# One core, three transformer layers in split float32: other order of the work in the seams, in the gated recurrence and at the start

## Chip, core and metric

The kernel runs on one core of one Trainium2 chip. The metric is the device time of one execution in microseconds (us); the figure for a kernel is the median of its runs.

## What is computed

256 tokens of width 1024 (x) go through three blocks. Block one: a gated linear recurrence (HGRN2) and a squared-ReLU MLP. Block two: differential attention on shared keys and values, and an MLP. Block three: latent attention beside a short convolution, a gated MLP, and a gated per-layer embedding. All is float32. The core of the reference, cut:

```python
h = x + rms_norm(hgrn2_mixer(rms_norm(x, a_norm_pre), a_w_in, lb, ...), a_norm_post)
h = h + rms_norm(squared_relu_mlp(rms_norm(h, mlp_norm_pre[0]), w_up, w_down), mlp_norm_post[0])
k_sh, v_sh = shared_kv(h, kv_norm, w_kv)
# differential attention + MLP in the same pattern, then the third block in the same pattern

# the recurrence, per head, per chunk of 64 tokens:
b = cumsum(log_f); o_inter = (q * exp(b)) @ state
scores[t, s] = sum_k q[t, k] * exp(b[t, k] - b[s, k]) * k[s, k]   # s <= t
o = o_inter + scores @ v
state = exp(b_last) * state + (k * exp(b_last - b)).T @ v
```

## The kernel before

Every large product is made in three parts. A float32 matrix is split into a high part (rounded by ScalarE, in fp32r) and a low part (what is left, made by VectorE), and TensorE sums high x high, low x high and high x low. A weight matrix comes in units of 256 output columns; each unit is loaded in two halves of 512 rows (a quantum: 128 x 1024 numbers). For each quantum SyncE issues a 512 KB DMA into `w_raw`, ScalarE copies it to `w_hi` (line 1350), VectorE subtracts (`w_lo`, line 1899), TensorE uses it. There are 4 raw and 5 converted slots; `raw_in`, `hi_ready`, `lo_ready` and `w_used` are the counters that pass a slot on. Each engine runs its own list in program order; the lists are written out by hand, and nothing else sets the order.

TensorE's inner loop is `quantum` (line 600). Its form "feat" makes one record of 512 columns (a high weight tile against the high and low parts of x, which lie side by side) and one of 256 columns (low weight tile); the form "one_bank" makes three records of 256 columns. A record in the trace is one MATMUL; a product of plain float32 operands shows as two records.

Three places matter here.

The seams. After each of six row-normalised products (`a_post`, `m0_post`, `b_post`, `m1_post`, `mix_post`, `f_post`) the residual stream `h` is renewed tile by tile (8 tiles of 128 rows): VectorE in `post` (line 2024) weighs, adds and makes the low part of the next product's input (`xs`, line 2035), ScalarE makes the high part (line 1442), and TensorE starts the next product tile by tile for two units at once. Until the first tile is there it runs seven products whose result nobody reads (`keep_streaming`, line 777). For tile 0 the high records (`high_records`) of both units come first and wait for the high part alone; the low ones (`low_records`) follow. From tile 1 on, all records of a tile wait for `xs_ready`, the low part. After the eight tiles TensorE sums the squares for the norm of the old entry in two places (`sums("kv_b")`, `sums("f_pre")`); these squares are folded on VectorE (`fold_squares`, `fold_again`), after it has converted two more weight quanta.

The recurrence. The 64 x 64 decays of a chunk are built over levels of blocks of 1, 2, 4 ... 64 tokens. For four heads at a time (a quad) there are nine steps: two on the undecayed q (even and odd tokens), six on decayed q (`hqd`), one for the pair of chunks. A step is 8 products `hk` x q with 64 columns (the last: 4 with 128), and stands behind one weight quantum: steps 0 to 8 behind quanta 9 to 17, steps 9 to 17 behind quanta 18 to 26 (`step`, line 833; `take_step`, line 2182). VectorE takes a step's scores under a mask into `acc` (lines 2201 and 2208) and decays q; GpSimd decays k and multiplies the forget gates (`fprod`).

The start. x comes in two halves; TensorE turns the first into PSUM, runs three products on a table that comes from memory (`keep_streaming(3, bank=2)`, after a wait for `tab_in`), and then turns the second. The first two units follow, with their parts mixed; then `setup_rest` (line 797) with the sum for the first norm and small products for tables; then quantum 4.

Of the kernel before, what the change touches and what calls it, by code (L numbers as in the profile page):

```python
# [8 lines left out]
F32 = mybir.dt.float32  # L9
F32R = mybir.dt.float32r  # L10
I32 = mybir.dt.int32
U32 = mybir.dt.uint32
# [29 lines left out]
STEPS = 8  # L42
T_FREQ = T_LEVEL + STEPS * CHUNK
# [6 lines left out]
def shape_tables():  # L50
# [8 lines left out]
    for n in range(STEPS):  # L59
        if n < 2:  # L60
            mask = (s // 2 == c) & (s % 2 <= n) if n else s == 2 * c
        else:
            b = 2 ** (n - 1)
            mask = (s // (2 * b) == c // b) & (s % (2 * b) < b)
        t[:, T_LEVEL + n * CHUNK:T_LEVEL + (n + 1) * CHUNK] = mask
# [99 lines left out]
HGRN_QUANTA = 32  # L165
AHEAD_FROM = 9
FIRST_STEP, QUAD_STEPS = 9, 9
# [44 lines left out]
def layered_kernel(nc, a, out):  # L212

    ctx = ExitStack()
    with ctx:
# [57 lines left out]
        hq = over("hq", [P, HEADS, S], F32, 0)  # L273
        hk = over("hk", [P, HEADS, S], F32, K8)
        hqd = over("hqd", [P, HEADS, S], F32, 2 * K8)
# [110 lines left out]
        lvl_scored, lvl_taken = sem("lvl_scored"), sem("lvl_taken")  # L386
        oh_ready, oh_squared, oh_ms, oh_guess = sem("oh_ready"), sem("oh_squared"), sem("oh_ms"), sem("oh_guess")
# [57 lines left out]
        def _(sp):  # L445
# [39 lines left out]
            for n in range(4):  # L485
                for which in range(2):
                    for part in range(2):
                        load("f0", (2, 0), 2 * n + which, part,
                             rows(a["a_w_in"][0], 4 * P * part, 4, D * (1 - which) + 256 * n, 256))
                        if n + which + part == 0:  # L490
                            load_x(1)
# [79 lines left out]
        def _(pe):  # L571
            mm = nc.tensor.matmul

            def high_records(s, x, kind, pset):

                hi, lo = w_hi[:, s, 0:2 * P], w_lo[:, s, 0:2 * P]
                for n in range(2):
                    w = slice(n * P, (n + 1) * P)
                    o_ap = ps[:, 2 * pset + n, 0:S] if kind == "feat" else ps[:, pset, n * S:(n + 1) * S]
                    mm(o_ap, hi[:, w], x[:, 0, 0:S], start=(kind == "feat" or n == 0), stop=False)  # L580
                    mm(o_ap, lo[:, w], x[:, 0, 0:S], start=False, stop=False)

            def low_records(s, x, kind, pset):

                for n in range(2):
                    o_ap = ps[:, 2 * pset + n, S:2 * S] if kind == "feat" else ps[:, pset, n * S:(n + 1) * S]
                    mm(o_ap, w_hi[:, s, n * P:(n + 1) * P], x[:, 0, S:2 * S], start=False, stop=False)

            def tile_zero(name, u, x, kind, psets):

                for b in range(2):
                    pe.wait_ge(lo_ready, 2 * (u + b) + 1)
                    if b == 0:
                        pe.wait_ge(xs_hi, XS0[name] + 1)
                    high_records(slot_of(u + b, 0), x, kind, psets[b])
                pe.wait_ge(xs_ready, XS0[name] + 1)
                for b in range(2):
                    low_records(slot_of(u + b, 0), x, kind, psets[b])
# [64 lines left out]
            def first_two_by_tile(name, xname, x, waits, after, between={}):  # L663
# [3 lines left out]
                tile_zero(xname, u, x, "feat", [(p + b) % 2 for b in range(2)])  # L667
                for k in range(1, KT):
                    for b in range(2):
                        if k == 4:  # L670
                            pe.wait_ge(lo_ready, 2 * (u + b) + k // 4 + 1)
                        if b == 0:
                            waits(k, 1)
# [2197 lines left out]
```

## Time and profile before

| | us |
|---|---|
| median of 3 runs | 1008.73 (1008.53 to 1009.54) |
| the profiled execution's own time | 1008.68 |
| its span (first to last instruction) | 1006.9 |
| TensorE matmul busy | 989.4 (98%) |
| VectorE / ScalarE / GpSimd busy | 742.1 / 554.5 / 74.0 |
| DMA | 166.47 MB, mean 165 GB/s |

Times in the rows below are from the span's start. A matmul's end is modelled, so records overlap: the pace of a row of like records is read from start to start, not from the length of one. The number in brackets behind a row is idle time of its engine before it, and what ended it.

### The profile page before, as it was taken

The page shows a single profiled execution, that of the slowest core. Times are in us where ns is not written, and L with a number is a line of the kernel's source. Part 1 is how long each engine was busy: PE and PEld are TensorE (multiplying, and loading weights), DVE is VectorE, ACT ScalarE, POOL GpSimd, SP SyncE. Part 2 cuts the span into 40 slices and gives each one's busy share as a digit, 9 for nine tenths or more (in the row PEclk, how much of TensorE's full clock was granted, in tenths as well). Part 3 has the DMA queues.
Part 4 walks back from the last instruction along what each step waited for, and adds up shares of the span by engine and source line. Part 5 has one row for each costly group of instructions (what it writes and reads, how often), then busy time and mean ns, then how long its engine had stood idle before and what let it go on. Part 6 is the DMA issues. An engine that isn't in the chain of part 4 may idle for free.

```text
span 1006.9 us, 16557 instructions
## 1 busy us (share of the span) xinstructions
PE 989.4 (98%) x6605; PEld 898.8 (89%) x6605; DVE 742.1 (74%) x1115; ACT 554.5 (55%) x819; POOL 74.0 (7%) x81
## 2 busy tenths in 40 slices
PE   7999999999999999999999999999999999999998
PEld 7999998888888989898888888999998788888897
DVE  5887677977764498766987844479777987776776
ACT  5943256655554475755655544455556665556444
POOL 6323101000201000001000201000001000000000
PEclk9999999999999999999999999999999999999999
DMA  8643435566656836435476565626526467665551
GB/s 262 189 133 114 126 112 161 161 204 182 192 183 187 259 110 197 137 115 154 141 218 186 172 199 184 183 76 177 180 85 187 127 182 202 185 186 181 177 166 42
DMA packets 164716, 166.47 MB, mean 165 GB/s; under 512 B 6784, under 2 KB 162832, under 8 KB 164640
## 3 DMA queue, kind: packets, MB, share of 16 engines
q1 hardware_dynamic: 162752, 163.47, 53.0%
q0 software_dynamic: 1056, 1.16, 0.5%
q8 instruction: 53, 0.87, 0.4%
q10 hardware_dynamic: 832, 0.79, 0.3%
q14 instruction: 23, 0.19, 0.1%
HBM read 163.79 MB, written 1.08 MB: 164 GB/s over the span
## 4 chain that ended last, share of the span: by engine, by line
PE 87%; DVE 7%; issue 2%; ACT 2%; POOL 1%; DMA 1%; ACTq 0%; DVEq 0%; POOLq 0%
PE ps L633 32%; PE ps L632 16%; PE ps L616 4%; PE ps L617 4%; PE ps L618 4%; PE ps L629 3%; PE ps L862 3%; PE ps L612 3%; PE ps L610 3%; PE ps L611 3%; DVE w_lo L1899 2%; PE ps L630 2%; PE ps L623 1%; PE ps L624 1%; PE ps L625 1%
## 5 line engine op out<-in xcount | busy, mean ns | idle before, releaser
L1899 DVE TENSOR_TENSOR w_lo<-w_raw,w_hi 128x1024 fp32r<-128x1024 f32 (+3 forms) x318 | 379.1, 1200 | 138.4 <-ACT w_hi L1350 136.7
L1350 ACT ACTIVATE w_hi<-w_raw 128x1024 fp32r<-128x1024 f32 x302 | 317.6, 1054 | 207.9 <-PE ps L633 94.3
L633 PE MATMUL ps<-xs,w_hi 128*128 128x512 f32 x840 | 296.5, 396 | 0.0
L632 PE MATMUL ps<-xs,w_lo 128*128 128x256 f32 x840 | 235.1, 280 | 2.0 <-DVE xs L2035 1.5
L633 PEld LDWEIGHTS ps<-xs,w_hi 128*128 128x128 f32 x840 | 157.7, 188 | 35.1
L633 PE MATMUL ps<-us,w_hi 128*128 128x512 f32 x498 | 176.3, 397 | 0.0
L632 PEld LDWEIGHTS ps<-xs,w_lo 128*128 128x128 f32 x840 | 158.3, 188 | 4.9 <-DVE xs L2035 2.1
L632 PE MATMUL ps<-us,w_lo 128*128 128x256 f32 x498 | 139.9, 281 | 0.0
L633 PEld LDWEIGHTS ps<-us,w_hi 128*128 128x128 f32 x498 | 93.6, 188 | 22.7
L616 PE MATMUL ps<-xs,w_hi 128*128 128x256 f32 x376 | 108.9, 290 | 1.2 <-DVE xs L2035 1.1
L617 PE MATMUL ps<-xs,w_hi 128*128 128x256 f32 x376 | 106.3, 283 | 0.0
L618 PE MATMUL ps<-xs,w_lo 128*128 128x256 f32 x376 | 106.3, 283 | 0.0
L632 PEld LDWEIGHTS ps<-us,w_lo 128*128 128x128 f32 x498 | 93.5, 188 | 0.3
L1357 ACT ACTIVATE tmp<-ps 128x512 f32<-128x512 f32 x75 | 44.5, 594 | 76.5 <-PE ps L633 76.4
L1927 DVE TENSOR_TENSOR mo<-ps,tmp 128x512 f32<-128x512 f32 x75 | 51.6, 688 | 41.3 <-ACT tmp L1357 41.3
L616 PEld LDWEIGHTS ps<-xs,w_hi 128*128 128x128 f32 x376 | 72.0, 191 | 2.8 <-DVE xs L2035 1.5
L2810 POOL TENSOR_TENSOR sq<-sq 128x512 f32<-128x512 f32 x12 | 20.1, 1672 | 716.6 <-ACT sq L1408 522.7
L617 PEld LDWEIGHTS ps<-xs,w_hi 128*128 128x128 f32 x376 | 72.0, 192 | 0.1
L618 PEld LDWEIGHTS ps<-xs,w_lo 128*128 128x128 f32 x376 | 71.9, 191 | 0.0
L612 PE MATMUL ps<-us,w_lo 128*128 128x256 f32 x172 | 48.3, 281 | 0.0
L610 PE MATMUL ps<-us,w_hi 128*128 128x256 f32 x172 | 48.3, 281 | 0.0
L611 PE MATMUL ps<-us,w_hi 128*128 128x256 f32 x172 | 48.3, 281 | 0.0
(412 smaller groups left out, 1684.2 us busy)
## 6 DMA issues: line engine op xcount, KB each, us to landing
w_raw<-in_mlp_w_up SPq DMA_DIRECT2D x64, 512.0 KB, 4.4
w_raw<-in_mlp_w_down SPq DMA_DIRECT2D x64, 512.0 KB, 3.6
w_raw<-in_a_w_in SPq DMA_DIRECT2D x32, 512.0 KB, 3.8
w_raw<-in_w_gate SPq DMA_DIRECT2D x22, 512.0 KB, 3.8
w_raw<-in_w_up SPq DMA_DIRECT2D x22, 512.0 KB, 4.5
w_raw<-in_w_down SPq DMA_DIRECT2D x20, 512.0 KB, 3.5
w_raw<-in_w_kv SPq DMA_DIRECT2D x16, 512.0 KB, 4.4
w_raw<-in_w_in SPq DMA_DIRECT2D x16, 512.0 KB, 3.9
```

The costliest lines, as they stand in the source:

```text
L610: mm(ps[:, bank, 0:S], hi[:, kk, w], x[:, kt, 0:S], start=first, stop=False)
L611: mm(ps[:, bank, 0:S], hi[:, kk, w], x[:, kt, S:2 * S], start=False, stop=False)
L612: o = mm(ps[:, bank, 0:S], lo[:, kk, w], x[:, kt, 0:S], start=False, stop=last)
L616: mm(ps[:, pset, at], hi[:, kk, w], x[:, kt, 0:S], start=first and n == 0, stop=False)
L617: mm(ps[:, pset, at], hi[:, kk, w], x[:, kt, S:2 * S], start=False, stop=False)
L618: o = mm(ps[:, pset, at], lo[:, kk, w], x[:, kt, 0:S], start=False, stop=last and n == 1)
L632: mm(ps[:, bank, 0:S], lo[:, kk, w], x[:, kt, 0:S], start=False, stop=False)
L633: o = mm(ps[:, bank, :], hi[:, kk, w], x[:, kt, :], start=False, stop=last)
L1350: o = fn(dst, raw, ACT.Copy)
L1357: o = fn(tmp[0:rows_, pset if slot is None else slot, :, :], ps[0:rows_, 2 * pset:2 * pset + 2, S:2 * S], ACT.Copy, scale=scale)
L1899: return v.tensor_tensor(d, x, y, ALU.subtract)
L1927: return v.tensor_tensor(dst, ps[0:rows_, 2 * pset:2 * pset + 2, 0:S], tmp[0:rows_, pset if slot is None else slot, :, :], ALU.add)
```

## The change

1. `two_by_tile` takes the place of `tile_zero` and the loops behind it, in the seams: for every tile, not the first alone, the high records of both units wait for the high part and come first, the low ones wait for the low part. In the form "feat" the record of 512 columns becomes two of 256 for tiles 1 to 7.
2. `keep_streaming` runs six products, not seven, at the six seams.
3. `sums("kv_b")` comes one quantum later and `sums("f_pre")` one quantum later; on VectorE the folds move between the two weight conversions at the seam's end.
4. The recurrence: q and decayed q now lie in one buffer `hq_both`. Ten uses of a PSUM bank in eight steps per quad: two steps hold two uses of 4 products with 128 columns each (even columns from q and odd ones from decayed q; then the odd diagonal from a moved copy of q together with level 2), the others stay as they are. The steps begin behind quantum 10. The first eight units come in the order f0 f1 q0 q1 f2 f3 q2 q3, and ScalarE takes the gates in pairs.
5. The start: three products of 128 columns on the identity that is there already, without the wait for `tab_in`; the first unit goes through all tiles before the second; `setup_rest` comes after quantum 4 and the turning of the first norm's factor after quantum 6. ScalarE and VectorE turn the second half of x before the next weights.

```diff
-                pe.wait_ge(tab_in, 16)
-                keep_streaming(3, bank=2)
+                for _ in range(3):
+                    mm(ps[:, 2, 0:P], ident, ident, start=True, stop=True)
...
-            for b, k2 in ((0, 0), (0, 1), (0, 2), (1, 0), (1, 1), (0, 3), (1, 2), (1, 3)):
-                part = k2 // 2
-                pe.wait_ge(lo_ready, 2 * b + part + 1)
...
-            setup_rest()
+            for b in range(2):
+                for k2 in range(4):
+                    part = k2 // 2
+                    if k2 % 2 == 0:
+                        pe.wait_ge(lo_ready, 2 * b + part + 1)
...
+            def two_by_tile(name, u, x, kind, psets, between={}):
+                for k in range(KT):
+                    tile = XS0[name] + (k if name in BY_TILE else k // 2) + 1
+                    for b in range(2):
+                        if k % 4 == 0:
+                            pe.wait_ge(lo_ready, 2 * (u + b) + k // 4 + 1)
+                        if b == 0:
+                            pe.wait_ge(xs_hi, tile)
+                        high_records(slot_of(u + b, k // 4), k, x, kind, psets[b])
+                    pe.wait_ge(xs_ready, tile)
+                    for b in range(2):
+                        o = low_records(slot_of(u + b, k // 4), k, x, kind, psets[b])
...
-                if q == 5:
+                if q == 4:
+                    setup_rest()
+                if q == 6:
                     turn_rstd("x")
                 if FIRST_STEP <= q < FIRST_STEP + 2 * QUAD_STEPS:
-                    step(q - FIRST_STEP)
+                    for n in uses_of(q - FIRST_STEP):
+                        use(n)
...
+                elif u < 4:
+                    for hh in range(2):
+                        hd = 4 * quad + 2 * (u % 2) + hh
+                        for tile in range(2):
+                            at = (2 * hh + tile) * P
+                            o_ap = ps[:, bank, at:at + P]
+                            if u < 2:
+                                rhs = both_q(hd, tile * P, [[2, CHUNK], [HEADS * S + 1, 2]])
+                                o_ap = o_ap.rearrange("p (a s) -> p a s", s=2)
+                            else:
+                                rhs = both_q(hd, tile * P + 2, [[4, P // 4], [HEADS * S, 2], [1, 2]])
+                                o_ap = o_ap.rearrange("p (g x j) -> p g x j", x=2, j=2)
+                            o = mm(o_ap, hk[:, hd, tile * P:(tile + 1) * P], rhs, start=True, stop=True)
...
-            keep_streaming(7)
-            stream("gu", xs, pairs=22, waits=xs_wait("f"), after=lambda: sums("f_pre"), two=True)
+            keep_streaming(6)
+            stream("gu", xs, pairs=22, waits=xs_wait("f"), mid=lambda: sums("f_pre"), two=True)
...
                 low_tile(KT - 1)
                 lo(following + 1, part=1)
+                if entry is not None:
+                    fold_squares(entry)
+                    fold_again()
                 lo(following + 2, part=0, in_seam=True)
```

TensorE's list at the first seam (behind `a_out`), before: two sums of squares, the seven unread products, tile 0 (lines 580, 581 high, 587 low), then tile 1 (632 low weight, 633 high weight with both parts of x).

```order
L762 MATMUL ps<-sq,table 128x256
L764 MATMUL ps<-sq,table 128x256
L779 MATMUL ps<-table 128x256 x7
L580 MATMUL ps<-xs,w_hi 128x256
L581 MATMUL ps<-xs,w_lo 128x256
L580 MATMUL ps<-xs,w_hi 128x256
L581 MATMUL ps<-xs,w_lo 128x256
L580 MATMUL ps<-xs,w_hi 128x256
L581 MATMUL ps<-xs,w_lo 128x256
L580 MATMUL ps<-xs,w_hi 128x256
L581 MATMUL ps<-xs,w_lo 128x256
L587 MATMUL ps<-xs,w_hi 128x256 x4
```

The same place after the change (its lines are numbered otherwise: 592 and 593 are the high records, 600 the low ones):

```order
L792 MATMUL ps<-table 128x256 x6
L592 MATMUL ps<-xs,w_hi 128x256
L593 MATMUL ps<-xs,w_lo 128x256
L592 MATMUL ps<-xs,w_hi 128x256
L593 MATMUL ps<-xs,w_lo 128x256
L592 MATMUL ps<-xs,w_hi 128x256
L593 MATMUL ps<-xs,w_lo 128x256
L592 MATMUL ps<-xs,w_hi 128x256
L593 MATMUL ps<-xs,w_lo 128x256
L600 MATMUL ps<-xs,w_hi 128x256 x4
L592 MATMUL ps<-xs,w_hi 128x256
L593 MATMUL ps<-xs,w_lo 128x256
```

Behind the four low records of tile 0 the high records of tile 1 now follow (the last two rows) where whole tiles stood.

VectorE's list at the end of the seam before the keys (`post("m0_post")` and what follows), before: the last low part of `xs`, two weight conversions, the two folds, and low parts for the queries' input.

```order
L2035 SCALAR_TENSOR_TENSOR xs<-h,vec,xs 128x256 x2
L1899 TENSOR_TENSOR w_lo<-w_raw,w_hi 128x1024 x2
L1997 TENSOR_TENSOR sq<-sq 128x1024
L2000 TENSOR_TENSOR sq<-sq 128x512
L2020 SCALAR_TENSOR_TENSOR xs_b<-h,vec,xs_b 128x256 x4
```

And after the change (lines 2044, 1908, 2006, 2009 and 2029 answer to 2035, 1899, 1997, 2000 and 2020):

```order
L2044 SCALAR_TENSOR_TENSOR xs<-h,vec,xs 128x256 x2
L1908 TENSOR_TENSOR w_lo<-w_raw,w_hi 128x1024
L2006 TENSOR_TENSOR sq<-sq 128x1024
L2009 TENSOR_TENSOR sq<-sq 128x512
L1908 TENSOR_TENSOR w_lo<-w_raw,w_hi 128x1024
L2029 SCALAR_TENSOR_TENSOR xs_b<-h,vec,xs_b 128x256 x4
```

The folds come one conversion earlier, and the second conversion two folds later.

## Rows read from the trace of the kernel before

**Rows 1.** The page: span, engines' busy time, granted clock in 40 slices

```profile
span 1006.9 us, 16557 instructions
PE 989.4 (98%) x6605; PEld 898.8 (89%) x6605; DVE 742.1 (74%) x1115; ACT 554.5 (55%) x819; POOL 74.0 (7%) x81
PEclk9999999999999999999999999999999999999999
```

**Rows 2.** Timeline of PE, up projection: start, length, engine, line, records

```profile
180.09 0.39 PE L633 MATMUL ps<-xs,w_hi 128*128 128x512 f32 x1
...
183.91 0.39 PE L633 MATMUL ps<-xs,w_hi 128*128 128x512 f32 x1
```

**Rows 3.** Timeline of PE, the start of the program

```profile
5.34 1.97 PE L793 MATMUL ps<-table,mo 128*128 128x128 f32 x8
8.08 2.93 PE L779 MATMUL ps<-table 128*128 128x256 f32 x6 [0.77 <-DMA table<-in_tables]
10.80 1.69 PE L793 MATMUL ps<-table,mo 128*128 128x128 f32 x8
12.25 0.36 PE L616 MATMUL ps<-xs,w_hi 128*128 128x256 f32 x1
...
23.84 0.59 PE L771 MATMUL ps<-sq,table 128*128 128x256 f32 x2
...
26.02 0.39 PE L616 MATMUL ps<-xs,w_hi 128*128 128x256 f32 x1
```

**Rows 4.** Issues of DMAs: KB each, us to landing (median of two)

```profile
mo<-in_x SPq DMA_DIRECT2D x2, 512.0 KB, 5.9
```

**Rows 5.** Timeline of VectorE, 25 to 34 us

```profile
25.40 0.42 DVE L1980 TENSOR_SCALAR ms<-ps 128x256 f32<-128x256 f32 x1 [1.23 <-ACT guess L1414]
...
33.05 1.23 DVE L1899 TENSOR_TENSOR w_lo<-w_raw,w_hi 128x1024 fp32r<-128x1024 f32 x1
```

**Rows 6.** Groups of the recurrence, 40 to 150 us, by shape: busy, mean ns

```profile
L862 PE MATMUL ps<-hq,hk 128*128 128x64 f32 x64 | 7.8, 272 | 0.2
L2208 DVE COPY_PREDICATED acc<-table,ps 128x512 f32<-128x512 uint32 x12 | 9.9, 829 | 15.1 <-PE ps L862 14.9 <-DVE hq L2153 0.2
L2201 DVE COPY_PREDICATED acc<-table,ps 128x512 f32<-128x512 uint32 x4 | 5.3, 1331 | 1.7 <-PE ps L862 1.7
```

**Rows 7.** Chain of waits, two steps of the recurrence: start, length, records

```profile
54.19 1.73 PE ps L862 x16
...
82.45 0.89 PE ps L851 x8
```

**Rows 8.** Timeline of the first seam, PE, then DVE and ACT

```profile
169.87 3.19 PE L779 MATMUL ps<-table 128*128 128x256 f32 x14
173.02 0.36 PE L580 MATMUL ps<-xs,w_hi 128*128 128x256 f32 x1
...
174.10 0.74 PE L587 MATMUL ps<-xs,w_hi 128*128 128x256 f32 x4
175.35 0.39 PE L632 MATMUL ps<-xs,w_lo 128*128 128x256 f32 x1 [0.51 <-DVE xs L2035]
...
174.82 0.48 DVE L2035 SCALAR_TENSOR_TENSOR xs<-h,vec,xs 128x256 fp32r<-128x256 f32 x1
...
172.37 0.51 ACT L1442 ACTIVATE xs<-h,vec 128x256 fp32r<-128x256 f32 x1 [0.46 <-DVE h L2040]
173.68 0.51 ACT L1442 ACTIVATE xs<-h,vec 128x256 fp32r<-128x256 f32 x1 [0.81 <-DVE h L2040]
```

**Rows 9.** Timeline of PE before the two late sums of squares

```profile
371.51 0.28 PE L618 MATMUL ps<-xs,w_lo 128*128 128x256 f32 x1
372.67 0.67 PE L771 MATMUL ps<-sq,table 128*128 128x256 f32 x2 [0.88 <-DVE sq L2000]
...
795.07 0.39 PE L633 MATMUL ps<-xs,w_hi 128*128 128x512 f32 x1
796.53 0.67 PE L771 MATMUL ps<-sq,table 128*128 128x256 f32 x2 [1.06 <-DVE sq L2000]
```

More of the change, by code:

```diff
@@ L165, with uses_of @@
 HGRN_QUANTA = 32
+HEAD_UNITS = [(kind, 2 * half + j) for half in range(2) for kind in "fq" for j in range(2)]
 AHEAD_FROM = 9
-FIRST_STEP, QUAD_STEPS = 9, 9
+FIRST_STEP, QUAD_STEPS, QUAD_USES = 10, 8, 10
+def uses_of(n):
+    quad, j = divmod(n, QUAD_STEPS)
+    return [QUAD_USES * quad + u for u in (((0, 1), (2, 3))[j] if j < 2 else (j + 2,))]
 F_AT = {b: HEADS * (S - 2 * S // b) for b in (2, 4, 8, 16, 32, 64)}
@@ L483, in deep @@
                 times(4, body)
[L485 to L491, printed above, removed]
+            for n, (kind, j) in enumerate(HEAD_UNITS):
+                for part in range(2):
+                    load("f0", (2, 0), n, part, rows(a["a_w_in"][0], 4 * P * part, 4, D * (kind == "f") + 256 * j, 256))
+                    if n + part == 0:
+                        load_x(1)
             def i_and_g(i):
@@ L697, in stream @@
             def stream(name, x, kinds=("feat",), per=1, pairs=4, body_pairs=2, last_kt=KT - 1, waits=None,
[L698 removed]
+                       after=None, two=False, first_pair=None, between={}, between_tiles=None, mid=None):
                 direct = name in DIRECT_LAST
@@ L705, in body @@
                         if name in BY_TILE_FIRST:
-                            first_two_by_tile(name, BY_TILE_FIRST[name], x, waits, after, between)
+                            first_two_by_tile(name, x, after, between)
                         else:
@@ new lines, in use @@
+                if u == QUAD_USES - 1:
+                    for hh in range(4):
+                        hd = 4 * quad + hh
+                        o = mm(ps[:, bank, hh * P:(hh + 1) * P], hk[:, hd, 0:P], hqd[:, hd, P:S], start=True, stop=True)
+                elif u < 4:
[11 more added lines that the diff above has]
+                            o = mm(o_ap, hk[:, hd, tile * P:(tile + 1) * P], rhs, start=True, stop=True)
+                else:
+                    b = 2 ** (u - 2)
+                    for hh in range(4):
+                        hd = 4 * quad + hh
+                        for tile in range(2):
+                            at = (2 * hh + tile) * CHUNK
@@ L1010, in _ @@
                 diff_quantum(q)
+                if q == 4:
+                    sums("kv_b")
                 if q == 6:
@@ L1466, in _ @@
                 o.then_inc(xs_hi, 1)
-                hi(j // 2, part=j % 2)
+                if j == 0:
+                    hi(0, part=0)
+                elif j == 2:
+                    hi(0, part=1)
+            for q in range(2, 5):
+                hi(q // 2, part=q % 2)
             squares("x", h, h_first, 0)
@@ L2072, in _ @@
                 o.then_inc(xs_ready, 1)
-                lo(j // 2, part=j % 2)
+                if j == 0:
+                    lo(0, part=0)
+                elif j == 2:
+                    lo(0, part=1)
+            for q in range(2, 4):
+                lo(1, part=q % 2)
             for g in range(4):
```

283 lines of the change are left out of this document (130 added, 153 removed).

## Prediction

> **What bounds the kernel now.** I read the page first: TensorE is busy for 989.4 of 1006.9 us and its granted clock is full in all slices, while VectorE has a quarter of the span free and ScalarE almost half [rows 1]. So the time is TensorE's list and its few holes; a change gains what it takes off that list or what hole it closes, and loses where it makes TensorE wait. Since the lengths of matmuls are modelled, I then read the timeline of TensorE from start to start. In the up projection 11 pairs of one record with 512 and one with 256 columns take 183.91 - 180.09 = 3.82 us, 0.347 a pair [rows 2]. The first two units are 96 records of 256 columns between 12.25 and 23.84: 0.121 each [rows 3]. Whatever is far above such a pace is a hole. Last come the views of the other engines at the holes, for who is late.
>
> **The seams, tile by tile.** At the first seam the four low records of tile 0 start at 174.10; at 0.12 each they are through at about 174.68 (the first one took 0.1 longer), and tile 1 starts at 175.35: a hole of 0.67 us [rows 8]. VectorE's low part of tile 1 ended it: it begins at 174.82 and lasts 0.48. The high part of tile 1 was there at 173.68 + 0.51 = 174.19. After the change eight high records, 8 x 0.12 = 0.96, start at 174.68 and end at 175.64, when the low part (175.30) is already there. Later tiles come every 1.25 us from VectorE (from the same two lines, 175.30 less 174.05) and take TensorE 12 x 0.12 = 1.44, so no later hole opens. The pattern stands in the timeline at all six seams, between 0.61 and 0.70: I take off 6 x 0.67 = **4.0**. The split of the 512 record costs: tiles 1 to 7 of two units with two blocks are 28 pairs, each 3 x 0.12 = 0.36 in place of 0.347 [rows 2, 3]; in the five seams and places with that form (`up0`, `b_out`, `up1`, `gu`, `pg`) 5 x 28 x up to 0.013 = 1.8, and nothing if the split halves pace as their sum. The extra weight load has the room of a 256 record. I take half, **+0.9**.
>
> **One unread product fewer.** Seven are 14 records from 169.87 to about 172.9, 0.216 a record, so one product is 0.43 us [rows 8]. The high part of tile 0 comes at 172.37 + 0.51 = 172.88 and the first high record starts at 173.02. With six, TensorE is free at 172.45 and waits for the same event: **0**. The low part of tile 0 ends the next wait in any case. If the clock fell in that hole of 0.57 us it would cost; the hole between tiles 0 and 1 is as long now, and no slice of the granted clock shows a fall [rows 1].
>
> **The two sums that waited.** `sums("kv_b")` starts 372.67 where the record before it started at 371.51, and `sums("f_pre")` 796.53 after 795.07; less the pace of 0.12 and 0.23 these are holes of 1.04 and 1.23 us, both ended by VectorE's second fold [rows 9]. One weight quantum of 2.8 to 2.9 us now lies between, and the fold comes a conversion earlier: both are covered. What is late next would be the second conversion, which now waits for the folds: the four operations keep their sum, so in the keys' seam it ends where the folds ended, at 372.67 at the latest [rows 9], and TensorE needs it one quantum after the tiles, at 371.51 + 0.12 - 0.67 + 2.9 = 373.9. It holds with 1 us to spare. **-2.25**, from 0 to -2.3.
>
> **The recurrence.** A step of 8 products with 64 columns is 16 records and takes 1.73 to 1.79 us on the chain, 0.108 to 0.112 a record; the step with 128 columns, 8 records, takes 0.89 [rows 7]. So a record of 128 columns costs what one of 64 does: what is paid is the weight load. Per quad three steps (48 records) become four uses of 4 products (32 records): 16 x 0.112 = 1.79 us, for two quads **-3.6**. The new operand alternates between q and decayed q 8 KB apart, which no row shows. From below: nothing is lost, since q with a column step of two is already read at 272 ns a record, as quickly as contiguous operands of the same size [rows 6]. From above: at 64 columns that would hide a read at half pace, so a record of 128 columns could take 0.22, and the 32 records of uses 0 and 1 would lose 3.4. I take the lower end, being nearest to the row. VectorE's masked copies that write every second column take 1331 ns, those that write blocks 829 in the mean [rows 6]; the merged ones write whole rows, so VectorE gets lighter there, and a moved copy of 256 columns is added ahead of the first decay. By my count of VectorE's list it ends about 1 us before TensorE needs it.
>
> The trace and the Trainium skill do not agree on strides for every engine. "SBUF — State Buffer", section "Door 1: The DMA port swizzle", says that accesses pay when they cross from one 16-byte line to the next and that at least two should fall in one line. By that rule uses 0 and 1 would pay, since neighbours lie in two buffers, while uses 2 and 3, which read in pairs, would not; VectorE's copies agree with it, TensorE's rows neither show nor exclude it, as a step of two still has two in a line.
>
> **The start.** x's halves are issued together and land after 5.9 us as the median of two [rows 4]; the first starts the transposes at 5.34, 4.6 us after its issue at 0.74, so the second lands after about 7.2, at 9.0. TensorE turns it only at 10.80, behind the three table products [rows 3]. After the change it can start at about 9.05: the short products are done at 8.3. But the pace of the start is half: 6 records from 8.08 to 10.80 are 0.43 each against 0.216 at the seam, so TensorE is at its 1.2 GHz level until about the first weight record at 12.25 [rows 3, 8]. If the rise comes at the same time, the first unit starts at 10.75, six records at 0.24 lose 0.7, and the two units are through at 22.95 where it was 23.84: **-0.9**. Each us by which the rise comes later costs half a us. Then quantum 4 (2.9), the setup products (26.02 - 23.84 = 2.2 [rows 3]), quanta 5 and 6, and the turned factor: TensorE wants quantum 7 at 34.0. VectorE's chain behind the sum of squares began at 25.40, 1.56 after it; it now begins at 25.85 + 1.56 = 27.4, and the conversion that stood 7.65 later, at 33.05 [rows 5], follows 1.2 earlier in it, since one conversion has moved ahead: 33.9 + 1.2 = 35.1. TensorE waits **+1.1** there. Old waits of the same stretch (three of 0.2 to 0.3, on weights, keys and decays) go, **-0.8**: gates and keys are now ready well before quantum 10 ends. What is queued behind quantum 7's conversion on VectorE are two keys' scalings (0.61 each) and quantum 8's conversion, just in time at 37.5 against 38.0.
>
> **The sum.** -4.0 + 0.9 + 0 - 2.25 - 3.6 - 0.9 + 1.1 - 0.8 = -9.6 us. Against the profiled execution's own 1008.68, which is the median of the runs to 0.05, that gives **999.1**. TensorE being the bound all through, a gain at one place should reach the end; where VectorE sets the pace for a while (third block's attention) its own chain starts from a product of TensorE and moves with it.
>
> **Rivals.**
> - *The alternating read is slow* (chance 0.14). 32 records at 0.22: +3.4, 1002.5. For it: VectorE's step-of-two copies; against: TensorE's step-of-two products run at full pace. The rule of the Trainium skill weighed above would give this result.
> - *The clock rises later at the start* (0.16). The unread products on the table were the longest run of TensorE before the rise; 6 records of 128 columns and a hole take their place. If it comes 4 us later, +2, and the wait at quantum 7 moves too: 1001.
> - *The seams give nothing* (0.12). ScalarE shares its queue between high parts, squares and a weight conversion; if it is late by more than 0.7, TensorE waits for the high part instead. The high part is there 1.1 us before the low one now [rows 8], which speaks against. Then 1003.
> - *Slower than before* (0.03). With six unread products the clock falls to 1.2 GHz in the holes of the six seams. Each us at that level costs 0.5; the 9.6 and the 2 to be slower need 3.9 us of half clock at each seam; a whole block of tiles (11.5 us) at half clock in all six would give 1033. Against: the hole is no longer than the one it replaces.
> - *It does only its merging* (0.05): the other parts meet other waits, 1005.
>
> **How the numbers follow.** The forecast, 997 to 1001, has 0.5. What a measurement of this kernel can tell from no change is about 0.2%, 2 us. Only the last two rivals come near or above 1006.7. Faster 0.93, same 0.04, slower 0.03. For 8 in 10 the range takes in the slow read and the late clock, and on the other side the split at no cost and no wait at quantum 7 (-2): **996.5 to 1003.5**.
>
> **What would show it.** In the new profile: no hole behind the low records of tile 0, six times; the sums of squares directly behind a record; a record of the merged uses at 0.107 to 0.112 from start to start (0.2 would be the first rival); the pace of the first unit's records changing from 0.24 to 0.12 near 12 us; a wait of about 1 us for `w_lo` near 34 us. Wrong would be the forecast if TensorE's waits for VectorE in the first 60 us add up to more than 3 us, or if the clock shows a fall.

## The result and the profile after

| | before | after |
|---|---|---|
| median | 1008.63 us (1008.11 to 1009.54, 4 runs) | 1001.41 us (1001.09 to 1001.74, 4 runs) |
| ratio | | 0.9928, 95% interval 0.991 to 0.9945 |
| the profiled execution | 1008.68, span 1006.9 | 1001.74, span 999.9 |

The kernel became 7.2 us faster; 9.6 were forecast (999.1, range 996.5 to 1003.5). The median of the kernel before is over one run more than in the table ahead of the prediction. From the page after, against [rows 1]: 96 records more, TensorE 5.5 us less busy, clock full.

```profile
span 999.9 us, 16744 instructions
PE 983.9 (98%) x6701; PEld 901.6 (90%) x6701; DVE 746.1 (75%) x1123; ACT 548.1 (55%) x814; POOL 75.8 (8%) x81
PEclk9999999999999999999999999999999999999999
```

Lines have moved: 779 is 792 (unread products), 580 and 581 are 592 and 593 (high), 587 is 600 (low), 616 to 618 are 640 to 642, 862 is 887 (878 for the merged uses), 771 is 784, 972 is 987.

The waits of PE after (engine, tile, line, who ended it: us in total, times, longest). The waits for `xs` L2035 and for `sq` of [rows 8, 9] are gone; the first row of the seams now names ScalarE, and two new ones of about 1 us stand below it.

```profile
PE ps L592 <- ACT xs L1449: 1.9, 5, 0.4
PE ps L987 <- DVE aq L2412: 1.0, 1, 1.0
PE ps L640 <- DVE w_lo L1908: 0.9, 1, 0.9
```

The first seam after (timeline of PE, as [rows 8]): behind the low records of tile 0, at 171.13, the high ones of tile 1 follow after 0.58 us where it was 1.25; then every tile takes 1.44. The hole in front of the first high record has grown by the product that was taken out (to 0.56 us beyond the pace), and the way from the sums to that record, 165.73 to 170.05, is 4.32 us as before.

```profile
165.73 0.59 PE L775 MATMUL ps<-sq,table 128*128 128x256 f32 x2
...
166.90 2.75 PE L792 MATMUL ps<-table 128*128 128x256 f32 x12
170.05 0.36 PE L592 MATMUL ps<-xs,w_hi 128*128 128x256 f32 x1 [0.40 <-ACT xs L1449]
...
171.13 0.74 PE L600 MATMUL ps<-xs,w_hi 128*128 128x256 f32 x4
171.71 0.28 PE L592 MATMUL ps<-xs,w_hi 128*128 128x256 f32 x1
...
173.15 0.28 PE L592 MATMUL ps<-xs,w_hi 128*128 128x256 f32 x1
```

The start (as [rows 3]), and quantum 7:

```profile
5.94 1.97 PE L806 MATMUL ps<-table,mo 128*128 128x128 f32 x8
7.70 1.49 PE L801 MATMUL ps<-table 128*128 128x128 f32 x6
9.18 1.97 PE L806 MATMUL ps<-table,mo 128*128 128x128 f32 x8
10.79 0.56 PE L640 MATMUL ps<-xs,w_hi 128*128 128x256 f32 x1
...
33.61 0.38 PE L842 MATMUL ps<-table,rstd 128*128 128x128 f32 x2
34.93 0.39 PE L640 MATMUL ps<-xs,w_hi 128*128 128x256 f32 x1 [0.94 <-DVE w_lo L1908]
```

The merged uses: 16 records of uses 0 and 1 from 46.55 to 49.07 (0.166 us from start to start), 16 of uses 2 and 3 from 52.08 to 53.90 (0.120), 16 of a later level, 64 columns each, from 56.88 to 58.58 (0.106).

```profile
46.55 2.82 PE L878 MATMUL ps<-hq_both,hk 128*128 128x128 f32 x16
49.07 0.41 PE L640 MATMUL ps<-xs,w_hi 128*128 128x256 f32 x1
...
52.08 2.08 PE L878 MATMUL ps<-hq_both,hk 128*128 128x128 f32 x16
53.90 0.37 PE L640 MATMUL ps<-xs,w_hi 128*128 128x256 f32 x1
```

Where the 7 us came from, in starts of TensorE's records in the two traces (the last record starts at 1002.80 and 995.86, -6.94). "Left" is the change within each stretch; holes are what a gap has beyond the pace of its kind.

| stretch, up to | left | made of |
|---|---|---|
| sums of `a_post` | -2.97 | the start up to quantum 7, without its wait, -1.22, quantum 7's wait +1.18, old waits there -0.89, the recurrence's products -1.68, a hole at 145.59 and small ones -0.36 |
| sums of `m0_post` | -0.33 | the seam with its tiles -0.42 |
| sums of `b_post` | -1.23 | seam -0.77, `kv_b`'s wait -1.03, new wait at the first scores +1.10, `b_out` -0.37 |
| sums of `m1_post` | -0.57 | seam -0.42, ahead of the first high record -0.15 |
| sums of `mix_post` | -0.61 | seam -0.59, ahead of it -0.23, `mix_pre`'s sums wait +0.28 |
| sums of `f_post` | -1.17 | seam -0.59, `f_pre`'s wait -1.22, two new waits in `gu` +0.46 |
| the end | -0.06 | seam -0.52, new wait in `pg` +0.36 |

### The profile page after: what moved, and what is told of

Read it like the earlier page. It is cut to its first block, busy times and chain, and to the rows that moved or that the text cites. A ratio compares the mean times of both kernels' runs of the same rounds, so it can differ in the third digit from the quotient of the medians.

```text
span 999.9 us, 16744 instructions
## 1 busy us (share of the span) xinstructions
PE 983.9 (98%) x6701; PEld 901.6 (90%) x6701; DVE 746.1 (75%) x1123; ACT 548.1 (55%) x814; POOL 75.8 (8%) x81
## 3 DMA queue, kind: packets, MB, share of 16 engines
q0 software_dynamic: 1056, 1.19, 0.5%
## 4 chain that ended last, share of the span: by engine, by line
PE 86%; DVE 10%; issue 1%; ACT 1%; DMA 0%; ACTq 0%; DVEq 0%
PE ps L657 29%; PE ps L656 15%; PE ps L640 4%; PE ps L641 3%; PE ps L642 3%; DVE w_lo L1908 3%; PE ps L653 3%; PE ps L636 3%; PE ps L634 3%; PE ps L635 3%; PE ps L592 2%; PE ps L600 2%; PE ps L593 2%; PE ps L887 2%; PE ps L654 1%
## 5 line engine op out<-in xcount | busy, mean ns | idle before, releaser
L657 PE MATMUL ps<-xs,w_hi 128*128 128x512 f32 x728 | 257.1, 396 | 0.0
L656 PE MATMUL ps<-xs,w_lo 128*128 128x256 f32 x728 | 203.5, 280 | 0.0
L657 PEld LDWEIGHTS ps<-xs,w_hi 128*128 128x128 f32 x728 | 136.7, 188 | 30.3
L656 PEld LDWEIGHTS ps<-xs,w_lo 128*128 128x128 f32 x728 | 137.1, 188 | 2.2
L640 PE MATMUL ps<-xs,w_hi 128*128 128x256 f32 x320 | 92.8, 290 | 0.9 <-DVE w_lo L1908 0.9
L641 PE MATMUL ps<-xs,w_hi 128*128 128x256 f32 x320 | 90.6, 283 | 0.0
L642 PE MATMUL ps<-xs,w_lo 128*128 128x256 f32 x320 | 90.5, 283 | 0.0
L640 PEld LDWEIGHTS ps<-xs,w_hi 128*128 128x128 f32 x320 | 61.4, 192 | 2.2 <-DVE w_lo L1908 1.2
L641 PEld LDWEIGHTS ps<-xs,w_hi 128*128 128x128 f32 x320 | 61.4, 192 | 0.1
L642 PEld LDWEIGHTS ps<-xs,w_lo 128*128 128x128 f32 x320 | 61.4, 192 | 0.0
L592 PE MATMUL ps<-xs,w_hi 128*128 128x256 f32 x192 | 48.5, 285 | 1.9 <-ACT xs L1449 1.9
L634 PE MATMUL ps<-us,w_hi 128*128 128x256 f32 x172 | 48.3, 281 | 0.0
```

The lines of the kernel that those rows point to most:

```text
L592: mm(o_ap, hi[:, w], x[:, kt, 0:S], start=kt == 0 and (kind == "feat" or n == 0), stop=False)
L634: mm(ps[:, bank, 0:S], hi[:, kk, w], x[:, kt, 0:S], start=first, stop=False)
L640: mm(ps[:, pset, at], hi[:, kk, w], x[:, kt, 0:S], start=first and n == 0, stop=False)
L641: mm(ps[:, pset, at], hi[:, kk, w], x[:, kt, S:2 * S], start=False, stop=False)
L642: o = mm(ps[:, pset, at], lo[:, kk, w], x[:, kt, 0:S], start=False, stop=last and n == 1)
L656: mm(ps[:, bank, 0:S], lo[:, kk, w], x[:, kt, 0:S], start=False, stop=False)
```

## The experiments

Each of e1 to e9 is the changed kernel with one edit and was run once; e10 and e12 join several. One run's time says little about differences under 1 us: the changed kernel itself took 1000.57 to 1001.82 in five runs (e11). So I also give the length of the stretch that the edit touches, from starts of TensorE's records in the trace. It repeats to 0.15 us: from the sums of `m0_post` to those of `b_post` eight executions with no edit there take 119.22 to 119.36.

### e1: the alternating read

```diff
-  rhs = both_q(hd, tile * P, [[2, CHUNK], [HEADS * S + 1, 2]])
-  o_ap = o_ap.rearrange("p (a s) -> p a s", s=2)
+  rhs = both_q(hd, tile * P, [[HEADS * S + 1, 2], [2, CHUNK]])
+  o_ap = o_ap.rearrange("p (a s) -> p s a", s=2)
```

> Uses 0 and 1 read the same 128 columns, but 64 of one buffer with a step of two and then 64 of the other, and write them to every second column of the bank; the result is the same. In the changed kernel the 16 records of these two uses start 0.166 us apart, against 0.120 for uses 2 and 3 and 0.106 for the products of 64 columns. Theory, the change of buffer at every column is the price: the two groups of 16 records fall from 2.52 us to 16 x 0.106 to 0.120 = 1.7 to 1.9 each, and the kernel gains 2 x 0.7 = 1.4 us, 1000.0 by the median of 1001.4. Rival, the step of two over 128 columns, or writing every second column, is the price: then the records stay at 0.166 and the time at 1001.4.

999.04 us. The same columns in two blocks start 0.1135 us apart, not 0.166 (timeline of PE):

```profile
45.60 1.97 PE L878 MATMUL ps<-hq_both,hk 128*128 128x128 f32 x16
47.33 0.36 PE L640 MATMUL ps<-xs,w_hi 128*128 128x256 f32 x1
```

16 records take 1.73 us where they took 2.52, in both quads, and the stretch from the sums of "x" to those of `a_post` is 138.47 against 140.16: -1.69 (the rest of the 2.4 is an earlier start, see e11). Shown: the price was the order in which the columns are read, from one buffer and the other in turn, and not the step of two. The changed kernel writes its 128 results side by side and e1 writes them to every second column, so writing with a step of two costs nothing here.

### e2: eight patterns

> The operands of uses 0 to 3 are replaced by other columns of the same two buffers, a pattern for each group of 8 records, so the attention scores of the first four levels are other numbers; the count and size of the products stay. First quad: use 0 reads 128 neighbours; use 1 reads A0 B0 A1 B1 (step one, buffer changed at every column); use 2 reads every second column of one buffer; use 3 reads 128 neighbours written as groups of four. Second quad: use 0 as in the changed kernel (A0 B1 A2 B3, 0.166 us a record); use 1 every fourth column of one buffer; use 2 pairs of each buffer in turn, as in the changed kernel (0.120); use 3 four neighbours of each buffer in turn. Theory, what counts is how often the next column lies in another 16-byte line: neighbours and groups of four 0.106 (32 lines), step of two and pairs 0.120 (64), step of four and both alternations 0.166 (128). Rival, what counts is the jump to the other buffer: then step of two and step of four take 0.106, and only the two alternations take 0.166.

1000.32 us. Starts of 128-column records apart, in us:

| pattern | measured |
|---|---|
| neighbours; neighbours in fours | 0.112 |
| four of each buffer in turn | 0.112 |
| every second column of one buffer | 0.1135 |
| pairs of each buffer in turn | 0.120 |
| A0 B0 A1 B1 | 0.136 |
| A0 B1 A2 B3 (as changed) | 0.166 |
| every fourth column of one buffer | 0.227 |

```profile
82.62 3.30 PE L883 MATMUL ps<-hq_both,hk 128*128 128x128 f32 x16
85.56 0.48 PE L647 MATMUL ps<-w_hi,xs 128*128 128x256 f32 x1
```

(8 records of the changed pattern and 8 with a step of four: 2.94 us together.) The rival falls, since a step of four within one buffer is the slowest of all. My theory holds only in part: the step of four has one column in each 16 bytes and costs double the step of two, which has two; but at two columns per 16 bytes the order still matters (0.1135 in one buffer, 0.166 alternating), and so does which columns alternate (A0 B0 A1 B1, four used in each 16 bytes, 0.136). So how many columns of 16 bytes are used and the change of buffer both matter; I had A0 B0 A1 B1 and the step of four at 0.166 each. The rule of the Trainium skill that the prediction weighed ("SBUF — State Buffer", section "Door 1: The DMA port swizzle": at least two accesses in one 16-byte line) had the direction right for uses 0 and 1, and right that the pairs are nearly free.

### e3: joined records

```diff
+FUSE_FROM = {'m0': 1, 'm1': 5, 'f': 3, 'last': 5}
...
+                    if k >= FUSE_FROM.get(name, KT):
+                        for b in range(2):
...
+                                pe.wait_ge(xs_ready, tile)
+                            o = quantum(slot_of(u + b, k // 4), 4 * (k // 4), 1, KT - 1, x, kind, psets[b], kk0=k % 4)
```

> In four places the tiles behind some tile take the record of 512 columns again, high and low part in one, unit by unit: from tile 1 in up0 (the order before the change), from tile 5 in up1, from tile 3 in gu, from tile 5 in pg; b_out stays split. Theory, a tile of two units costs 12 x 0.120 = 1.44 us split and 8 records of 1.39 joined: up0 has its hole of 0.67 us behind tile 0 again and its seven tiles 0.35 faster, so it loses 0.3; up1 gains 3 x 0.05 = 0.15 without a hole, gu meets VectorE (low parts come every 1.25 us) in a wait of up to 0.4 us at tile 3; and since the first unit's last record is no longer held behind the second unit's high records, the wait of 0.46 us behind pg's first two units (982.61 in the changed kernel) falls to 0.1 as before. All in all within 0.3 us of 1001.4. Rival: the split costs nothing and the wait in pg has another cause; then the tiles take 1.44 us either way, and the wait stays.

1000.93 us. In `up0` the hole behind tile 0 is back (0.67 us), and its eight tiles take 12.33 us against 11.74. Joined tiles take 1.39 us in `gu` and 1.41 to 1.42 in `up0`, `up1` and `pg` of this run (in the kernel before 1.39 in `up0` and 1.42 in `gu`), split ones 1.44 everywhere: the split costs 0.02 to 0.05 a tile. Since they came down to 1.41 and not to 1.39, `up0` lost 0.50 us from the sums of `a_post` to those of `m0_post`, and not the 0.3 that I had expected. `gu` met VectorE at tile 3, 0.31 us. The wait behind `pg`'s first two units is gone, as expected (PE: changed, then e3):

```profile
982.28 0.60 PE L1283 MATMUL ps<-table,ple 128*128 128x128 f32 x4
983.18 0.50 PE L653 MATMUL ps<-xs,w_hi 128*128 128x512 f32 x1 [0.30 <-DVE mo L1936]
```

```profile
981.95 0.60 PE L1298 MATMUL ps<-table,ple 128*128 128x128 f32 x4
982.37 0.50 PE L668 MATMUL ps<-xs,w_hi 128*128 128x512 f32 x1
```

In the changed kernel the first unit's last low records stand behind the second unit's high ones, so its bank is copied later, and the next pair waits for it.

### e4: unread products

> The six seams get 7, 4, 2, 0, 8 and 5 unread products in place of 6 each. Theory: TensorE waits for ScalarE's high part of tile 0 in any case, 3.15 us after the start of the first unread product, so the first high record keeps its distance of 4.3 us from the sums of squares in all six, with a hole of 0.13 us at 7, 1.0 at 5, 1.4 at 4, 2.3 at 2 and 3.1 at none; 8 products end 0.3 us late. The clock stays full. Then the time is 1001.7. Rival: the clock falls in the longer holes; records behind it then start 0.24 us apart in place of 0.12, and each us of that costs half a us; a block of tiles (11.5 us) at that pace adds 11.5 us per seam, 1013 with one and 1036 with three.

1002.50 us. With 7, 4, 2 and 5 products (`a_post`, `m0_post`, `b_post`, `f_post`) the first high record stays 4.33, 4.32, 4.16 and 4.53 us behind the sums, where it is in the changed kernel, and the clock is full; eight (`mix_post`) end 0.11 late. With none, `m1_post`, it falls: the records after 661.2 start 0.213 apart for 3 us (windows of the trace: start and end, length, busy time and count of PE, PEld, DVE, ACT, POOL, granted clock, DMA share, GB/s).

```profile
657.00:660.00 3.00, 0.50 (x5) 0.26 (x3) 2.32 (x6) 2.01 (x6) 0.72 (x2) 1.00 0.62 171
661.20:664.20 3.00, 3.00 (x15) 3.00 (x15) 2.89 (x8) 1.95 (x5) 0.00 (x0) 0.50 0.01 3
```

Ahead of it TensorE had a hole of 2.7 us beyond its pace, and the fall came 1.1 us after it had taken up work again. The eight tiles took 13.17 in place of 11.81: +1.36. So six products cost nothing, as forecast, nor do two, where the hole is 2.3 us; the rival came true only at none.

### e5: the query ahead of two conversions

> VectorE scales the first query unit right behind the key unit before it, ahead of the two conversions for quanta 9 and 10; nothing else moves. In the changed kernel TensorE waits 1.19 us at 382.69 before the first scores, for the query unit that VectorE scales at 383.17, behind those conversions at 380.83 and 382.03. Theory, the holes that the change closed in front of it (0.67 at the seam and 1.04 at the sums) brought TensorE to the scores earlier while VectorE's list without gaps stayed as long, so most of it came back as this wait: with the query first the wait is gone (the scaling then ends at about 381.5), the conversions for quanta 9 and 10 are still there at 382.8 and 384.0, and from the sums before to b_post the stage takes 1.1 us less; 1000.3. Rival: VectorE is the bound of this whole stage and something later waits instead, quantum 9 or the second scores; then the stage takes as long as before and the time stays 1001.4.

999.97 us; the stretch from `m0_post` to `b_post` is 118.26 against 119.26: -1.00. The wait is gone, and none took its place. VectorE, then PE, of the changed kernel, and the same two of e5:

```profile
380.23 0.68 DVE L2408 TENSOR_TENSOR ak<-ps,rstd 128x512 f32<-128x512 f32 x1
380.83 1.22 DVE L1908 TENSOR_TENSOR w_lo<-w_raw,w_hi 128x1024 fp32r<-128x1024 f32 x1
382.03 1.21 DVE L1908 TENSOR_TENSOR w_lo<-w_raw,w_hi 128x1024 fp32r<-128x1024 f32 x1
383.17 0.68 DVE L2412 TENSOR_TENSOR aq<-ps,rstd 128x512 f32<-128x512 f32 x1
...
384.00 0.71 PE L987 MATMUL ps<-ak,aq 64*128 64x128 f32 x8 [1.02 <-DVE aq L2412]
```

```profile
380.24 0.68 DVE L2412 TENSOR_TENSOR aq<-ps,rstd 128x512 f32<-128x512 f32 x1
380.91 3.49 DVE L1908 TENSOR_TENSOR w_lo<-w_raw,w_hi 128x1024 fp32r<-128x1024 f32 x3
...
382.31 0.71 PE L987 MATMUL ps<-ak,aq 64*128 64x128 f32 x8
```

### e6: the small work later

> VectorE's copy of the relative bias (0.67 us) and the three small operations on the lambdas move from ahead of the first two units' scaling (31.97) to behind the keys of quantum 5. Theory, the wait of 1.10 us before quantum 7 (33.72 in the changed kernel) is VectorE's list behind the sum of squares alone: the conversion for quantum 7 comes 1.2 earlier, TensorE waits 0.1 at the most, and the products that follow (quantum 8 at 36.7, whose weights come at 35.8 or earlier) do not wait, so the time falls by 1.1 to 1000.3. Rival, another wait takes its place: ScalarE's high part for quantum 7 at 30.80 and the sigmoids behind it do not move, and quanta 8 to 10 or the first use of the recurrence wait instead; then the gain is under 0.4.

1000.09 us; from the sums of "x" to those of `a_post` 139.23 against 140.16: -0.93. Quantum 7 follows the turned factor directly. The theory holds, but for 0.17 us of the 1.10 expected, which went into holes of under 0.1.

### e7: the sums back at the end of the tiles

> The sums of squares kv_b and f_pre stand again directly behind the first two units, ahead of the next quantum; VectorE's folds stay a conversion earlier than before the change. Theory: the folds end at 368.1 in the changed kernel where TensorE is through with the tiles at 367.6, so the wait at kv_b is 0.5 to 0.6 us in place of 1.04, and the wait before the first scores shrinks by the same amount, since VectorE's list sets the end of both: the stage to b_post takes as long as in the changed kernel. At f_pre the wait is 0.6, and the stage takes 0.6 more minus what the waits of gu (0.26 and 0.20 in the changed kernel) give back. In all +0.3 to +0.6, 1001.9. Rival: the two are independent, then the full waits come on top, +1.2.

1001.89 us. `kv_b` waits 0.68 us beyond the pace, `f_pre` as long; the wait at the scores falls from 1.19 to 0.44, those in `gu` vanish. `m0_post` to `b_post`: 119.56 against 119.26; `mix_post` to `f_post`: 192.62 against 192.58, and 192.50 to 192.58 in all eight executions with no edit there. PE in e7:

```profile
368.16 0.67 PE L784 MATMUL ps<-sq,table 128*128 128x256 f32 x2 [0.52 <-DVE sq L2008]
...
383.91 0.71 PE L988 MATMUL ps<-ak,aq 64*128 64x128 f32 x8 [0.28 <-DVE aq L2411]
```

So putting the sums behind a quantum was worth 0.2 to 0.3 us at the first place and 0.04 to 0.12 at the second, where the wait in front of them had been 1.04 and 1.23 before the change. In both kernels the first scores start 32.5 us after the sums of `m0_post` (32.49 in e7, 32.48 as changed): up to there nothing is lost, as I had expected, because VectorE's list decides when that stage goes on. The 0.29 arise in holes of about 0.04 in the 22 us behind the first scores, which I had not expected and whose cause is open. At the second place the new wait of 0.68 less the two of `gu` that vanish (0.26, and 0.20 to 0.28) leaves 0.14 to 0.22, near what was measured.

### e8, e9, e11: the start

> Only the unread products ahead of x's second half are the old ones again: three with 256 columns on the table, which wait for the table, in place of three with 128 on the identity. Theory, this was the start's hold-up: they run from about 7.9 to 10.5, the second half is turned at 10.5 in place of 9.0, the first weight record starts at about 12.0 in place of 9.9 to 10.8, and the first six quanta end 1.2 to 1.9 later. Where the clock has risen by then, the records behind it take 0.12 from the first. The wait before quantum 7 moves along, so the whole kernel loses 1.2 to 1.9: 1002.6 to 1003.3. Rival: the first weights are the hold-up (in the runs with an early start a record waits for weights at 12.7); then at most 0.5 us is lost.

> The three unread products ahead of x's second half are left out altogether. In the runs so far that have them TensorE waits 0.2 to 0.6 us behind them for the second half, which is turned at 8.9 to 9.2, and the records get their full pace at 9.1 to 11.5. Theory, the second half's landing and the first weights set the start, and the products are only there to keep TensorE busy: the second half is turned at the same time, so if the clock rises at the same time the first six quanta end where they did (the sums of squares at 24.6 to 25.6). Rival, the idle stretch of 1.5 us puts the rise off: then the records keep 0.21 to 0.24 us for as much longer, and each us of that costs half a us, up to 1.5 us for the whole kernel (1003).

> The changed kernel as it is, on the same chip and beside the same runs of the kernel before as e10: 1001.4 and 0.993 of before. In its first profile the first product began 0.45 to 0.75 us later in the span than in seven of the eight others; if that was a chance of that execution, this profile has x's second half turned at about 9.0, the first weight record at 10.0 to 10.6 and the sums at 24.6 to 25.0, and a span of 999.3.

1003.08, 1002.42 and 1001.43 us (e11: 1000.57 to 1001.82 in 5 runs, ratio 0.992, 0.9907 to 0.9934). The sums of "x" start at 27.08, 26.39 and 25.48; in the first profile of the changed kernel at 25.57. PE in e8, e9 and e11:

```profile
8.10 2.93 PE L792 MATMUL ps<-table 128*128 128x256 f32 x6 [0.68 <-DMA table<-in_tables]
10.82 1.91 PE L806 MATMUL ps<-table,mo 128*128 128x128 f32 x8
12.39 0.56 PE L640 MATMUL ps<-xs,w_hi 128*128 128x256 f32 x1
```

```profile
8.86 1.97 PE L805 MATMUL ps<-table,mo 128*128 128x128 f32 x8 [1.51 <-DMA mo<-in_x]
10.48 0.56 PE L640 MATMUL ps<-xs,w_hi 128*128 128x256 f32 x1
```

```profile
9.09 1.31 PE L806 MATMUL ps<-table,mo 128*128 128x128 f32 x8
10.15 0.36 PE L640 MATMUL ps<-xs,w_hi 128*128 128x256 f32 x1
...
13.87 0.39 PE L640 MATMUL ps<-xs,w_hi 128*128 128x256 f32 x1 [0.61 <-DVE w_lo L1908]
```

e8: the old products hold the second half until 10.82, and 1.51 us are lost at the sums against the first profile, as expected. e9: x is turned just as early, but the records start 0.213 apart until 13.6, where the rise of the granted clock stood at 11.5 in the changed kernel: +0.82 at the sums. No execution with the products had its rise as late as 13.6, so the rival is right as far as one run can say: the idle stretch costs, and the products are needed. e11 began 0.15 us earlier than the first profile and its clock rose at 9.6, but it then waited 0.77 us for the second half of the first unit's weights and came out within 0.1. My reading of the first profile as a late one was wrong: a second limit, the weights, stands just behind the first. Over all eleven executions with the short products the granted clock rises between 8.3 (e10) and 11.5 and the sums start between 24.62 and 25.57; what moves the rise by 3 us stays open. A time taken once thus carries up to 1 us of the start's chance.

### e10 and e12: together

> The changed kernel with the reads of uses 0 and 1 in blocks (measured between 10.79 and the sums of a_post: -1.7 us), the query unit ahead of the two conversions (-1.0), the small work later (-0.9), and joined records of 512 columns from tile 5 on in up0, up1, gu and pg and in tile 7 of b_out, which also lets the first unit be copied before the second one's last records (pg's wait of 0.46 falls to 0.1: -0.36; 3 tiles by 0.025 to 0.05 at four places: -0.3 to -0.6). Theory, these are holes and costs at places of their own and add up: -4.3 to -4.6, 997.0 against the changed kernel's 1001.4. Rival: one shared slack, so that the gains do not add; VectorE's list after the seam of kv and the chain behind the sum of squares then wait for something common, and the sum is under 3 us, 998.5 or more.

997.86 us (997.48 to 998.04, 4 runs), ratio to before 0.9886 (0.9872 to 0.9899): 3.6 us under the changed kernel. In the traces the sums of "x" start 0.61 earlier than in e11 (24.88 and 25.48), which no edit explains; from there to the last record it is 2.83 us, so the rival (under 3) is nearer than the theory. Holes at places of their own would have given -4.3 to -4.6; most of what is missing is missing in one place: up to `a_post` the two edits give -1.80, alone they gave -1.69 and -0.93. With quantum 7 and uses 0 and 1 both quicker TensorE waits before uses 2 and 3 (PE, VectorE and GpSimd of e10):

```profile
50.36 2.16 PE L893 MATMUL ps<-hq_both,hk 128*128 128x128 f32 x16 [0.74 <-DVE hq_both L2210]
...
46.80 1.22 DVE L1923 TENSOR_TENSOR w_lo<-w_raw,w_hi 128x1024 fp32r<-128x1024 f32 x1
47.94 1.73 DVE L2229 COPY hq_both<-hq_both 128x256 f32<-128x256 f32 x1
49.58 0.68 DVE L2210 TENSOR_TENSOR hq_both<-hq_both,fg 128x512 f32<-128x512 f32 x1
...
46.91 2.50 POOL L2857 TENSOR_TENSOR hk<-hk,fg 128x512 f32<-128x512 f32 x1 [4.39 <-PE ps L893]
```

> e10 with one more edit: in the first quad VectorE's moved copy and first decay come ahead of the conversion that it did before them. In e10 TensorE waits 0.90 us at 49.34 for uses 2 and 3 (for VectorE's decay, 49.58 + 0.68, and GpSimd's, 46.91 + 2.50): uses 0 and 1 were through at 46.5, but the conversion ran until 48.0, and the copy of 0.40 us took 1.73 beside GpSimd's decay. Theory, the gains of e10 that were missing were eaten by this wait, which VectorE's order makes: with copy and decay first they are done by 49.3, GpSimd's decay takes 1.5 to 1.75 in place of 2.50, and the wait is 0.1 at the most; 0.8 us less than e10, 997.0. Rival, VectorE and GpSimd cannot work on their decays at the same time, so one stands behind the other whatever the order: 46.9 + 1.75 + 0.7 = 49.35 at the best and 50.2 if VectorE's operation is stretched to GpSimd's end; then 0.3 or less is gained.

998.79 us (998.22 to 999.81, 4 runs), 0.9902 (0.9886 to 0.9919): no gain. That wait is gone, and one of 1.46 us stands one level on (54.48), for the next decay, behind the two conversions that had given way. From the sums of "x" to `a_post` it takes 138.91, e10 138.36. Neither expectation has it: VectorE has no gap over 0.22 us from 46.3 to 56 in e12, so what is brought forward there pushes something else back. Over the whole kernel, from the sums of "x" to the last record, e10 and e12 differ by 0.15 us (967.28 and 967.13); by the median e10 is the fastest version.

## Why the prediction was right, and where its steps were not

- **Seams.** -4.0 for six holes: measured 3.90, from the first low record of tile 0 to the next tile (0.67, 0.67, 0.67, 0.61, 0.67 and 0.61). The split was put at +0.9, half of its upper bound; by the pace of the tiles it took nearly all of it where the old ones ran at 1.39. Net, the six seams gave -3.31, and `b_out` -0.37 where I had +0.2: it had a hole of 0.32 us of the same kind (460.55 before), which I had not counted.
- **Unread products.** 0, measured 0 in four seams, -0.15 and -0.23 in the other two; e4 shows it for 7, 5, 4 and 2 products as well.
- **Sums.** The step that failed: "both are covered". -2.25 at the place itself (measured -2.25), but I followed VectorE only to the next conversion. Counted from the sums of `m0_post`, VectorE's unbroken list begins to scale the query at 31.65 us in both kernels. TensorE came to the first scores at 33.2 before; after the change it is there at 31.3, and goes on at 32.5. So of 1.9 us closed ahead of it 1.1 came back as a longer wait there (e5 takes it away, e7 moves part of it to the sums); in `gu` 0.46 came back.
- **The recurrence.** The largest error: -3.6 forecast, -1.68 measured. Uses 0 and 1 cost 0.166 a record, between my two ends (0.112 and 0.22); I took the lower one because [rows 6] showed 64 columns with a step of two at full pace. That row could not tell: a step of two in one buffer is free even at 128 columns (e2), the alternation is not. 2 x 0.73 us by e1; the rest is that a step taken out was worth 1.70 us where I had 1.79, and pairs cost 0.120. So the first rival had the mechanism and half its price. One reading behind it was wrong: VectorE's copies do not agree with the rule of the Trainium skill that the prediction weighed ("SBUF — State Buffer", the same section), that two accesses in one 16-byte line are enough. The mean of 829 ns in [rows 6] mixes two kinds. The copy that writes pairs, two columns in each 16 bytes, takes 1.34 us, as long as those that write every second column (1.33), and the ones with blocks of four and more take 0.70 to 0.75 (VectorE before):

```profile
56.91 1.34 DVE L2208 COPY_PREDICATED acc<-table,ps 128x512 f32<-128x512 uint32 x1 [0.21 <-DVE hq L2153]
60.92 0.72 DVE L2208 COPY_PREDICATED acc<-table,ps 128x512 f32<-128x512 uint32 x1 [1.03 <-PE ps L862]
```

The change also puts VectorE's decay of q ahead of the masked copy in the later uses, which its list does not name; no run tests that alone.

- **Start.** -0.9 forecast for the end of the first two units, -1.15 measured (22.69 against 23.84), and 1.5 lost by undoing the products (e8). The rise of the clock, the second rival, came earlier (11.5 against 12.1), not later; e9 shows what it costs when it does.
- **Quantum 7.** +1.1 forecast, +1.18 measured; the reason, VectorE's list behind the sums, by e6.
- **Old waits.** -0.8 forecast, -0.89 measured.
- **Not foreseen:** `pg` +0.36 (e3 has the cause), `mix_pre` +0.28 (not tried), against it -0.38 ahead of two seams and -0.36 in the recurrence's last quanta.

The time is inside the range because these misses of both signs partly cancel, which is in part luck: +1.9 for the uses and +2.2 for waits that came back or were new, against -1.6 for what was better than forecast.

## What to carry to other kernels

A hole that is closed brings the bound engine early to the next place: follow the list of the engine that fed it, without a gap, until it has slack again, and ask there which item could go first. Bounds for an unseen operand pattern need a row with the same pattern; when the nearest row lets two ends stand, a probe of eight patterns in one run is cheap. Joining gains that were measured one by one also shows which of them share a limit: -1.7 (e1), -1.0 (e5), -0.9 (e6) and -0.5 (`pg` in e3) alone were -2.8 together, from the sums of "x" on.

## What the runs showed of the hardware

- A record with 128 fp32 columns of the moving operand takes 0.112 us as neighbours, 0.1135 with a step of two and 0.227 with a step of four; columns from two buffers in turn take 0.136 to 0.166, pairs in turn 0.120 (e2). Writing the result to every second column costs nothing (e1).
- VectorE's masked copy of 128x512 fp32 takes 1.33 us when it writes every second column or every second pair, and 0.70 to 0.75 in blocks of four and more (before).
- VectorE and GpSimd take longer side by side: the same copy took 0.40 us when it began just ahead of GpSimd's decay (VectorE's decay behind it then took 2.03 in place of 0.68, GpSimd's 1.75; changed kernel and e12), and 1.73 when it began during it (GpSimd's then took 2.50; e10). No run takes one of the two away.
- TensorE's clock fell to half (1.2 GHz) after a hole of 2.7 us, 1.1 us into the work that followed, and stayed there for 3 us (e4, once); holes up to 2.3 us left it at 2.4 GHz in the same run.
